# A mixture-of-experts decoder layer: accumulators by the parity of the expert, and scatters issued ahead of gathers

## The reference

```python
def _moe(xn, l, p):
    B, T, D = xn.shape
    x = xn.reshape(B * T, D)
    scores = jax.nn.sigmoid((x @ p['router_w'][l]).astype(jnp.float32))
    _, idx = lax.top_k(scores + p['router_bias'][l].astype(jnp.float32), TOP_K)
    sel = jnp.take_along_axis(scores, idx, axis=-1)
    wsel = sel / jnp.sum(sel, axis=-1, keepdims=True) * ROUTED_SCALE
    gates = jnp.sum(jax.nn.one_hot(idx, N_EXPERTS, dtype=jnp.float32) * wsel[..., None], axis=1).astype(x.dtype)
    hid = jax.nn.silu(jnp.einsum('nd,edf->nef', x, p['exp_w_gate'][l])) * jnp.einsum('nd,edf->nef', x, p['exp_w_up'][l])
    routed = jnp.einsum('nef,efd->nd', hid * gates[..., None], p['exp_w_down'][l])
    shared = (jax.nn.silu(x @ p['shared_w_gate'][l]) * (x @ p['shared_w_up'][l])) @ p['shared_w_down'][l]
    return (routed + shared).reshape(B, T, D)
```

## Time and profile before

| | |
|---|---|
| median of 3 runs | 945.3 us (943.29 to 945.57) |
| the profiled execution, its own time | 946.73 us |
| its span in the profile | 944.6 us |
| mean granted TensorE clock | 0.907 of full speed |
| TensorE matmuls busy | 765.5 us, 81% of the span |
| VectorE, ScalarE, GpSimd busy | 36%, 25%, 40% |
| DMA | 277.05 MB |
| expert loop | about 295 to 905 us |

### The profile page before, as it was taken

One profiled execution on the slowest core, in us unless ns is written; L12 is line 12 of the kernel. 1 busy time (PEld: TensorE's weight loads), 2 busy tenths in 40 slices (PEclk: granted clock), 3 DMA queues, 4 the chain that ended last, 5 costly groups with the idle time before them and its releaser, 6 DMA issues.

```text
span 944.6 us, 14829 instructions
## 1 busy us (share of the span) xinstructions
PE 765.5 (81%) x5228; PEld 431.2 (46%) x5229; DVE 340.7 (36%) x612; ACT 235.4 (25%) x409; POOL 380.3 (40%) x300
## 2 busy tenths in 40 slices
PE   1879999999988977997788888986879877878900
PEld 1657654645544533553355444553445433444400
DVE  2243355654632426232232232323323323232306
ACT  2112362212212322222222222222312222222202
POOL 0030000010250555654555645555655455555523
PEclk9979999998969988998899898999989988998955
DMA  9985936708223999999999999999989999898233
GB/s 260 400 289 157 346 118 247 267 26 342 100 71 143 396 393 398 347 352 351 386 326 381 370 388 326 349 399 382 370 306 389 377 368 372 288 389 298 49 75 140
DMA packets 85494, 277.05 MB, mean 293 GB/s; under 512 B 28355, under 2 KB 31859, under 8 KB 60476
## 3 DMA queue, kind: packets, MB, share of 16 engines
q1 hardware_dynamic: 50966, 250.88, 68.4%
q0 software_dynamic: 29216, 22.64, 10.9%
q10 hardware_dynamic: 5254, 2.76, 1.1%
HBM read 283.25 MB, written 39.00 MB: 341 GB/s over the span
## 4 chain that ended last, share of the span: by engine, by line
DMA 51%; PE 31%; issue 9%; DVE 6%; ACT 1%; POOL 1%; POOLq 1%; SPq 1%; DVEq 0%
DMA acc_rows<-et,idx 43%; PE bank L1072 5%; PE bank L794 4%; PE bank L802 4%; DMA et<-xn_rows,idx 3%; PE bank L937 3%; PE bank L821 3%; PE bank L1108 3%; DMA gu<-in_ada_w 3%; PE bank L779 2%; PE bank L1154 1%; PE bank L805 1%; DMA xn<-xn_rows,idx 1%; PE bank L943 1%; PE bank L1033 1%
## 5 line engine op out<-in xcount | busy, mean ns | idle before, releaser
L1072 PE MATMUL bank<-gu,et 128*64 128x256 f32 x2496 | 286.5, 385 | 5.2 <-ACT et L695 3.1
L1072 PEld LDWEIGHTS bank<-gu,et 128*64 128x64 f32 x2496 | 184.2, 140 | 132.7 <-issue 54.7
L1108 PE MATMUL bank<-dn,et 128*64 128x512 f32 x624 | 173.9, 691 | 8.6 <-issue 6.6
L459 POOL DMA_INDIRECT acc_rows<-et,idx x64 | 106.3, 1660 | 182.1 <-DMA acc_rows<-et,idx 139.3
L466 POOL DMA_INDIRECT acc_rows<-et,idx x64 | 101.0, 1578 | 65.2 <-issue 48.1
L1548 DVE COPY et<-bank 128x256 f32<-128x256 f32 x64 | 27.1, 424 | 218.0 <-PE bank L1089 214.7
L710 ACT ACTIVATE et<-bank,mb 128x512 f32<-128x512 f32 x64 | 44.0, 687 | 245.2 <-DMA acc_rows<-et,idx 202.7
L1108 PEld LDWEIGHTS bank<-dn,et 128*64 128x64 f32 x624 | 44.9, 153 | 86.0 <-issue 86.0
L1555 DVE TENSOR_SCALAR et<-bank,mb 128x512 f32<-128x512 f32 x64 | 48.0, 751 | 94.5 <-PE bank L1108 71.8
L1534 DVE COPY et<-bank 128x512 f32<-128x512 f32 x64 | 44.2, 691 | 102.3 <-PE bank L1055 101.8
L702 ACT ACTIVATE et<-bank 64x512 f32<-64x512 f32 x64 | 37.6, 588 | 140.5 <-PE bank L1072 140.5
(11 more groups left out here) (272 smaller groups left out, 702.4 us busy)
## 6 DMA issues: line engine op xcount, KB each, us to landing
gu<-in_exp_w_gate SPq DMA_DIRECT2D x64, 1024.0 KB, 7.6
gu<-in_exp_w_up SPq DMA_DIRECT2D x64, 1024.0 KB, 10.8
dn<-in_exp_w_down SPq DMA_DIRECT2D x64, 1024.0 KB, 9.1
gu<-in_ada_w SPq DMA_DIRECT2D x12, 2048.0 KB, 14.4
gu<-in_w_in SPq DMA_DIRECT2D x4, 2048.0 KB, 19.8
gu<-in_w_out SPq DMA_DIRECT2D x2, 2048.0 KB, 12.5
acc_rows<-dn SPq DMA_DIRECT2D x2, 1280.0 KB, 16.2
acc_rows<-et,idx POOLq DMA_INDIRECT x128
```

The source lines that it names most:

```text
L459: pool.indirect_dma_start(acc_rows[0], bass.IndirectOffsetOnAxis(ap=idx[:, u, 0:1], axis=0), yo[:, u % 2, 0, :], None, bounds_check=2 * T ...
L1072: mm = pe.matmul(bank[u % 2][64 * c:64 * c + 64, b * FE:(b + 1) * FE], xt[:, b, k % 4, k // 4, :], w[:, (c * KT + k) * FE:(c * KT + k + 1) ...
L1108: mm = pe.matmul(bank[5 + b][64 * c:64 * c + 64, :], hT[:, b, j, :], dn[:, dslot(u), j * D + c * HALF:j * D + (c + 1) * HALF], start=(j == ...
```

## The change

The accumulators are chosen by the parity of the expert and no longer by block: both scatters of an even expert add to `acc_rows[0]`, both of an odd one to `acc_rows[1]`. Before the first of them GpSimd waits until both scatters of e-2 have landed; between the two there is no wait for a transfer. Evacuation (`y0`, `y1`) waits for both scatters of e-2, before it waited for the one of its own block. `index` waits for expert e-8 by the new count. And in GpSimd's loop body the scatters of expert u-1 come first, then the gathers of expert u+3.

```diff
@@ scatter (GpSimd)
-                if not (isinstance(e, int) and e == 0):
-                    pool.wait_ge(scattered[0], 16 * e)
+                if not (isinstance(e, int) and e < 2):
+                    pool.wait_ge(scattered[u % 2], 16 * (e - u % 2))
                 pool.sem_inc(s["pool_go"], 1)
-                pool.indirect_dma_start(acc_rows[0], bass.IndirectOffsetOnAxis(ap=idx[:, u, 0:1], axis=0),
+                pool.indirect_dma_start(acc_rows[u % 2], bass.IndirectOffsetOnAxis(ap=idx[:, u, 0:1], axis=0),
                                         yo[:, u % 2, 0, :], None, bounds_check=2 * T - 1, oob_is_err=False,
-                                        compute_op=ALU.add).then_inc(scattered[0], 16)
+                                        compute_op=ALU.add).then_inc(scattered[u % 2], 16)
                 pool.wait_ge(s["y1_evac"], e + 1)
-                if not (isinstance(e, int) and e == 0):
-                    pool.wait_ge(scattered[1], 16 * e)
                 pool.sem_inc(s["pool_go"], 1)
-                pool.indirect_dma_start(acc_rows[1], bass.IndirectOffsetOnAxis(ap=idx[:, u, 1:2], axis=0),
+                pool.indirect_dma_start(acc_rows[u % 2], bass.IndirectOffsetOnAxis(ap=idx[:, u, 1:2], axis=0),
                                         yo[:, u % 2, 1, :], None, bounds_check=2 * T - 1, oob_is_err=False,
-                                        compute_op=ALU.add).then_inc(scattered[1], 16)
+                                        compute_op=ALU.add).then_inc(scattered[u % 2], 16)
@@ body (GpSimd)
                 for u in range(U):
+                    if not (first and u == 0):
+                        scatter(r, i if u else i - 1, (u - 1) % U)
                     if not (last and u >= U - AHEAD):
                         gather(r, i + (u + AHEAD) // U, (u + AHEAD) % U)
-                    if not (first and u == 0):
-                        scatter(r, i if u else i - 1, (u - 1) % U)
@@ y1 (ScalarE)
-                    act.wait_ge(scattered[1], 16 * e - 16)
+                    act.wait_ge(scattered[u % 2], 16 * (e - u % 2))
@@ index (VectorE)
-                    for b in range(2):
-                        dve.wait_ge(scattered[b], 16 * e - 16 * (U - 1))
+                    dve.wait_ge(scattered[u % 2], 16 * (e - u % 2) - 16 * (U - 2))
@@ y0 (VectorE)
-                    dve.wait_ge(scattered[0], 16 * e - 16)
+                    dve.wait_ge(scattered[u % 2], 16 * (e - u % 2))
```

## The result

The changed kernel takes 999.9 us (median of 4 runs, 992.63 to 1005.75) against 945.4 us beside it (943.29 to 951.28): ratio 1.056, 95% interval 1.048 to 1.065. Slower was forecast, with 956 us; 1000 lies outside the range of 936 to 976. So the sign came and the size didn't: +54 us where the sum said +10.8.

The account below looks back on a forecast made before the run. Scatters waiting on scatters were taken to bound the kernel, delaying gathers and TensorE. Loop +6.2, start +6.5 and end -1.9 us gave +10.8 on 946.7, so 957.5, as median 956 us; range 936 to 976.

Parts of the forecast that it names:

- the sum: Whole kernel: 6.2 us from the expert loop, 6.5 at the start, -1.9 at the end, +10.8 us in all.
- What bounds the kernel before: Expert loop: scatters waiting on scatters make GpSimd late, so gathers and TensorE's transposes are late; 9.72 us per expert.
- rival A: Expert loop: landings shorten, the two-expert loop doesn't bind, DMA engines set the pace; 928 us, chance 0.2.
- The new loop: Expert loop: the new GpSimd order closes a loop over two experts, 18.72 us, 9.36 each; before, it ran over three.
- The disputed term: In the two-expert loop, from the first gather's issue (L445) to the transposes: 10.8 us; it decides the sign.
- The start: First experts: gather 4 now stands behind both first scatters, so the row of experts starts one step later, +6.5 us.
- The step that failed: Two-expert loop: TensorE's down and transposes slowed by the mean granted clock of 0.92, adding 0.21 us per expert.
- the 2.57 us: Two-expert loop, TensorE's rows behind the wait: transposes to down 0.58 us and down to evacuation 1.99 us.
- Long experts: Two-expert loop: 14 of 64 experts are long, with extra down and transposes, adding 0.26 us per expert.
- rival B: Expert loop: even and odd experts bunch, TensorE's clock falls behind one long wait, transfers queue; 983 us, chance 0.16.
- Rival C: Expert loop: gathers set the same pace scatters did, slight DMA relief eats the start's loss; 943 to 948, chance 0.14.
- The end: Last experts: the last L459 is no longer held by the scatter of expert 62, -1.9 us.

Follow-up runs that it names:

- e1_acc_only: The changed kernel with the old GpSimd order, gathers ahead of scatters, so only the accumulators go by parity: 921.5 us, ratio 0.976.
- e3_gather_between: The changed kernel with the two gathers issued between the expert's two scatters: 942.5 us, ratio 0.996.
- e6_ahead4: The changed kernel with AHEAD = 4 instead of 3, scatters still first: 919.9 us, ratio 0.973.
- e13_short: The changed kernel with no expert taken as long, so TensorE leaves out the second blocks (output differs): 988.7 us, ratio 1.048.
- e15_short_fill12: The changed kernel with no long experts, plus 12 filling matmuls ahead of TensorE's waits for gathers: 951.3 us, ratio 1.008.
- e8_quarter_gu: The changed kernel loading only the first quarter of each expert's gate and up weights (output differs): 915.0 us, ratio 0.970.
- e5_fill8: The changed kernel, long experts kept, with 8 filling matmuls ahead of TensorE's waits for gathers: 1029.2 us, ratio 1.089.
- e14_short_fill8: The changed kernel with no long experts, plus 8 filling matmuls ahead of TensorE's waits for gathers: 971.4 us, ratio 1.029.
- e7_acc_ahead4: The changed kernel with the old GpSimd order, gathers ahead of scatters, and AHEAD = 4: 917.7 us, ratio 0.971.

## Why the prediction was right in sign and wrong in size

**What bounds the kernel before** was read rightly. The scatter behind scatter goes (no wait for `acc_rows` in 320 to 870 us), and taken away alone this is worth 24 us, where rival A has 17: e1_acc_only's 921.5 against 928.

**The new loop** is the one that was laid out: down, evacuation, two scatters, two gathers, landing, transposes, down, over two experts. It makes 46 of the 55 steps of the way back; e3_gather_between took 1.9 us of issue out of it and was 57 us faster than the change; e6_ahead4 opened it and the loss was gone.

**The disputed term** was sized rightly. L445 to the transposes was 11.05 in the turn shown, 10.83 in the 23 turns, 10.4 in the mean of all 31 cases of 57 in which the transposes began within 0.5 us of the landing; forecast 10.8. The fear that a landing depends on what else stands in GpSimd's queue did not come true in this loop: 8.4 us (L448) to 9.1 us (L445) in the median, by the semaphore events that the trace holds. No loop's median came near the 2.6 us that I estimated from the Trainium skill (DMA: Bandwidth & Descriptors, "Anatomy of one DMA — SWDGE (gpsimd) path"); the trace has such a landing, 2.3 us, once the weight stream has ended, and with less of that stream the median was 4.6.

**The start** was right: +7.2 for +6.5. Expert 5's transposes at 324.86 and expert 4's at 316.06, where the forecast said near 324 for expert 4. With the stretch before 6.2 us shorter that is 317.7, and it came 1.6 us earlier still, 11.15 us after its gather:

```profile
304.91 1.34 POOL L445 DMA_INDIRECT et<-xn_rows,idx  x1 [0.30 <-issue]
...
316.06 1.11 PE L1053 MATMUL bank<-ident,et 128*128 128x128 f32 x4 [6.46 <-issue]
```

The granted levels show here too: 1.11 us for these four matmuls, behind a wait of 6.46.

**The step that failed** is this one: "in a loop that goes through down and transposes right after TensorE stood still, 16% of 2.6 us, halved, is 0.21". The sentence says itself what makes the product wrong. The 16% are a mean over all of TensorE's time, but the loop passes through TensorE only behind the wait, and there the clock is at the lower of its two levels: down to evacuation of a short expert takes 3.39 us in the mean where the transposes ahead of it began at the landing, and 2.20 where not. In the turn shown the 2.57 us are then not lengthened by 16% but by 2.06 (1.04 for 0.58, 3.59 for 1.99), and in the mean of the 23 turns by 2.07: 1.03 per expert, five times the term. With it the sum is 9.36 + 1.03 + 0.26 = 10.65, and the measured pace is 10.61. That sum agrees better than it may, since not every step lies in the loop. e13_short to e15_short_fill12 show the clock's part by experiment: with the clock held the same two rows shrink by 2.0 us a turn, and the pace by 0.77 us (10.56 to 9.79) although 2.8 us of work per expert were added. That 0.77 is less than 1.0, because gather to transposes grew and TensorE's own steps began to bind.

**The second part of the same step**: the sum takes one loop alone. There are two, of even and odd experts, on one TensorE. They fall into pairs, one long wait and one step without (446.38, 454.87, 467.85, 475.85), and in 26 of 57 experts the gathers had landed and TensorE came late, with a mean of 12.7 us from gather to transposes. The way back tells what of the excess is which. Its 55 steps take 581.8 us, the forecast has 9.83 for each, 540.7: of the 41.1 us between them, 32.4 lie in the 23 turns (21.07 for 19.66, the forecast's two experts with its terms for clock and long experts) and 8.6 in the nine steps of TensorE. Six of these follow a long expert and take 11.6 to 13.0 us; the sum's 0.26 for long experts counts only their rows in the loop.

**Long experts** were taken at 0.26 us per expert; their leaving gave 0.05 (10.61 to 10.56). Their work falls in part into TensorE's wait, and the granted clock is lower without them, 0.82 instead of 0.88.

**The rivals.** What happened is rival B, which had 0.16. Its signs were a pace over 10.2 and a clock under 0.9, and they came (10.61 and 0.891 over the span), with the bunching and the half clock behind one long wait. The forecast named this mechanism and had only the 0.21 for it in its own sum. Nor was B's price worked out from these signs: it took 983 from a longer landing, which did not come. Had it doubled the 2.57 us behind the wait in every turn, as 1.2 for 2.4 GHz does, it would have said 956 + 56 x (1.29 - 0.21) = 1016, an upper end with the measured time inside. Rival A's time is nearly what the accumulators alone do, but its mechanism isn't shown: the DMA share was the same before, e8_quarter_gu has the pace of e1_acc_only (9.27) at a share of 0.74, and the scatters stayed on e1_acc_only's chain, at 20% of it. Rival C did not come.

**The end**: +0.8 for -1.9. The last L459 is no longer held (0.30 us of idle time before it, at 956.73), as forecast; but from expert 61's transposes to the last down it takes 33.95 us instead of 29.17. Why stays open; it is small either way.

## What to carry to other kernels

Count how many experts (steps) a closed loop through a queue spans before and after a reordering; here it went from three to two with no wait added. Price what a closed loop does right behind a long wait of TensorE at 1.2 GHz, not at the mean clock. And where two independent chains share one engine, expect them to bunch into one long wait and none, and test a new order with a longer lead before judging it (AHEAD = 4 turned +5.6% into -2.7%).

## What the runs showed of the hardware

- Added matmuls can make such a kernel faster: 12 of 128x128 per expert (2.8 us at full clock) took e13_short from 988.7 to 951.3 us. With the long experts in, 8 of them made the changed kernel slower (999.9 to 1029.2).
- TensorE at a granted clock of 0.50 to 0.56 does eight matmuls of down in 3.31 to 3.68 us instead of 1.94, and the gap between two weight loads doubles with them, 0.62 instead of 0.29 us.
- The landing of the same gather has a median of 4.6 us at a DMA share of 0.74 (e8_quarter_gu) and 8.4, 9.2, 9.2 and 8.9 at 0.90, 0.93, 0.96 and 0.99 (e5_fill8, e13_short, e14_short_fill8, e15_short_fill12, all with the scatters first and a lead of three). It is 12.6 in e6_ahead4 (0.99, at most 15.4) and e7_acc_ahead4 (0.98), and 14.7 for the first gather in e1_acc_only (0.98), but 9.0 in the kernel before at the same 0.98. So it isn't a matter of the share alone; what makes the difference between 9 and 14 us is open. In the two with a lead of four TensorE waited at most 2.0 us in all at its transposes, so there the longer landing cost nothing.
